# One core of Trainium2, hybrid decoder step: order of the first page and modulation loads

## What is computed

```python
def adaln_modulation(c, w_ada, b_ada):
    m = jnp.einsum('nd,de->ne', jax.nn.silu(c), w_ada) + b_ada
    return jnp.split(m[:, None, :], 6, axis=-1)

# decoder_layer, shortened
shift_m, scale_m, gate_m, shift_f, scale_f, gate_f = adaln_modulation(c, lw['w_ada'], lw['b_ada'])
h = rmsnorm(x, lw['g_norm_mix']) * (1.0 + scale_m) + shift_m
p = jnp.einsum('ntd,de->nte', h, lw['w_in'])
...
# mla_sample: keys of the cached pages and their norms
c_all = jnp.concatenate([pool_c[pages_i].reshape(PAST_LEN, KV_LORA), c_i], axis=0)
k = mla_keys(c_all, kr_all, w_uk, g_qk_k)      # k_nope = c_kv @ w_uk, then RMSNorm per head
...
x = x + gate_m * merged @ w_out
x = x + gate_f * moe_ffn(rmsnorm(x, g_norm_ffn) * (1 + scale_f) + shift_f)   # 64 experts, top 8, and one shared
```

## Time and profile before

| | us |
|---|---|
| median of 3 runs | 1010.48 (1009.39 to 1010.88) |
| the profiled execution | 1010.36 |
| its span in the profile | 1008.6 |
| TensorE busy | 972.6 (96%) |
| VectorE busy | 610.6 (61%) |
| ScalarE busy | 188.0 (19%) |
| DMA, moved | 311.86 MB, mean 309 GB/s |

### The profile page before, as it was taken

How to read it: one execution, slowest core, us unless ns; L and a number is a source line. 1 busy time by engine, 2 the same in 40 slices (tenths; PEclk the granted TensorE clock), 3 DMA queues, 4 the chain that set the end, 5 groups by cost and what they waited for, 6 DMA issues and landing times.

```text
span 1008.6 us, 14072 instructions
## 1 busy us (share of the span) xinstructions
PE 972.6 (96%) x4542; PEld 547.3 (54%) x4542; DVE 610.6 (61%) x1563; ACT 188.0 (19%) x385; POOL 56.6 (6%) x81
## 2 busy tenths in 40 slices
PE   6999999999999999999999999999999999999997
PEld 2487766444447788888744344444444444344443
DVE  3513322468754011123749889889888888888875
ACT  3311231335435100002510010000000000000000
POOL 0100010000000000000210000000000000000000
PEclk9999999999999999999999999999999999999999
DMA  8994469655545483544569999999999999999991
GB/s 314 421 402 186 175 228 322 180 164 169 162 125 235 160 356 132 209 159 176 214 244 415 425 424 424 426 421 419 423 428 422 422 427 420 425 422 421 422 393 61
DMA packets 54921, 311.86 MB, mean 309 GB/s; under 512 B 8922, under 2 KB 28410, under 8 KB 32978
## 3 DMA queue, kind: packets, MB, share of 16 engines
q1 hardware_dynamic: 48546, 297.21, 74.0%
q0 software_dynamic: 6320, 13.93, 3.9%
HBM read 315.80 MB, written 3.95 MB: 317 GB/s over the span
## 4 chain that ended last, share of the span: by engine, by line
PE 73%; DMA 20%; DVE 3%; issue 1%; SPq 1%; ACT 0%; DVEq 0%; PEldq 0%
PE bank L747 48%; DMA ring<-in_w_e_gu 18%; PE pA L747 17%; PE pB L747 4%; PE pC L747 3%; DMA pT<-in_poolT 1%; PE pD L747 1%; PE pA L782 1%; DMA ring<-in_w_br 0%; PE pA L991 0%; SPq L592 0%; DVE xT L2327 0%; PE pC L1000 0%; PE bank L1315 0%; DVE xT L2403 0%
## 5 line engine op out<-in xcount | busy, mean ns | idle before, releaser
L747 PE MATMUL pA<-ring,qT 128*64 128x512 f32 x992 | 226.8, 595 | 11.1 <-DMA ring<-in_w_e_gu 11.0
L2315 DVE STREAM_TRANSPOSE qT<-xs 32x256 f32<-32x256 f32 x480 | 209.2, 436 | 7.7
L747 PE MATMUL bank<-hT,ring 128*128 128x264 f32 (+1 forms) x832 | 189.3, 388 | 0.9 <-PE bank L747 0.9
L747 PEld LDWEIGHTS bank<-hT,ring 128*128 128x128 f32 (+1 forms) x832 | 154.3, 189 | 34.4 <-issue 8.7
L747 PEld LDWEIGHTS pA<-ring,qT 128*64 128x64 f32 x992 | 74.0, 137 | 137.7 <-issue 128.8
L747 PE MATMUL bank<-pT,vtok 128*128 128x264 f32 x512 | 127.9, 393 | 0.3 <-DVE pT L2407 0.3
L747 PEld LDWEIGHTS bank<-pT,vtok 128*128 128x128 f32 x512 | 92.0, 190 | 39.3 <-issue 26.7
L2324 DVE TENSOR_TENSOR pT<-pT,bank 128x264 f32<-128x264 f32 x248 | 99.9, 427 | 8.8 <-PE bank L747 7.3
L747 PE MATMUL bank<-wuk,ring 128*128 128x512 f32 x192 | 86.3, 597 | 0.0
L747 PE MATMUL pB<-ring,oaT 128*64 128x512 f32 x244 | 62.0, 605 | 0.0
L747 PE MATMUL pC<-ring,oaT 128*64 128x512 f32 x244 | 60.3, 592 | 0.0
(11 more groups left out here) (344 smaller groups left out, 795.0 us busy)
## 6 DMA issues: line engine op xcount, KB each, us to landing
ring<-in_w_e_gu SPq DMA_DIRECT2D x62, 2048.0 KB, 18.9
ring<-in_w_e_dn SPq DMA_DIRECT2D x61, 1024.0 KB, 18.6
ring<-in_poolT SPq DMA_DIRECT2D x64, 208.0 KB, 2.7
ring<-in_w_ada SPq DMA_DIRECT2D x12, 1024.0 KB, 9.6
ring<-in_w_bg SPq DMA_DIRECT2D x4, 3072.0 KB, 11.6
ring<-in_w_mix SPq DMA_DIRECT2D x5, 2048.0 KB, 8.7
ring<-in_w_ada SPq DMA_DIRECT2D x4, 2048.0 KB, 12.5
ring<-in_poolR SPq DMA_DIRECT2D x56, 128.0 KB, 2.1
```

What stands on the lines that cost most here:

```text
L747: return nc.tensor.matmul(out, lhsT, rhs, start=start, stop=stop)
L2315: last = V.transpose(xTs[32 * j:32 * j + 32, q % 2, :, 32 * a:32 * a + 32], src[32 * a:32 * a + 32, j])
```

## The change

The first half of modulation chunk 0 (4 of its 8 blocks, 1 MB) is issued ahead of SyncE's wait for the page table and counts on the semaphore of page 0, together with w_uk; the second half goes out after pages 0 to 5, and alone counts on `wgt[0]`. Page groups become {0}, {1}, {2, 3}, {4, 5}, {6, 7}, {8 to 11}, {12 to 15}. Banks follow a table of their own (`EBANK`), as the groups of pages no longer fit the stages. On TensorE, ScalarE and VectorE pages 4 and 5 move ahead of chunk 0 and of the norm's square and tile sums.

```diff
-EGROUP = (0, 1, 4, 6, 8, 10, 12, 16)
+EGROUP = (0, 1, 2, 4, 6, 8, 12, 16)
+EBANK = (0, 4, 6, 8, 10, 12)
...
-STAGES = [("ek0", 1), ("ek1", 3), ("ada0", 1), ("ek4", 2), ("ek6", 2), ("norm1", 1), ("ada1", 1), ("ek8", 2), ("ada2", 1),
+STAGES = [("ek0", 4), ("ek4", 2), ("ada0", 1), ("ek6", 2), ("norm1", 1), ("ada1", 1), ("ek8", 2), ("ada2", 1),
...
 def early_bank(e):
-    g = max(x for x in EGROUP if x <= e)
+    g = max(x for x in EBANK if x <= e)
...
             def ada_item(x):
+                if x == 0:
+                    sp.dma_start(part(0, CT * 512, CT, 512), A["w_ada"][0][:, CT:DT]).then_inc(wgt[0], 16)
+                    return
...
             sp.dma_start(wuk, A["w_uk"]).then_inc(d_early[0], 16)
+            sp.dma_start(part(0, 0, CT, 512), A["w_ada"][0][:, 0:CT]).then_inc(d_early[0], 16)
             sp.wait_ge(d_ptab, 16)
-            early_pages(0)
-            early_pages(1)
+            for g in range(4):
+                early_pages(g)
             ada_item(0)
             sp.dma_start(xT[:], A["xT"]).then_inc(d_in, 16)
             sp.dma_start(vec[:], A["vec"]).then_inc(d_in, 16)
-            early_pages(2)
-            early_pages(3)
+            early_pages(4)
             ada_item(1)
-            early_pages(4)
+            early_pages(5)
             ada_item(2)
-            early_pages(5)
             early_pages(6)
             ada_item(3)
...
                     if e in EGROUP:
                         g = EGROUP.index(e)
-                        pe.wait_ge(d_early[g], 16 * (EGROUP[g + 1] - e + (g == 0)))
+                        pe.wait_ge(d_early[g], 16 * (EGROUP[g + 1] - e + 2 * (g == 0)))
...
-            early_keys(0, 2)
-            early_keys(2, 4)
+            early_keys(0, 6)
             pe.wait_ge(s["csilu"], 1)
             pe.wait_ge(d_late, 16)
             ada_item(0)
-            early_keys(4, 6)
             pe.wait_ge(s["consts"], 6)
             early_keys(6, 8)
...
-            early_squares(0, 4)
+            early_squares(0, 6)
             ada_rows((0,))
             act.wait_ge(d_in, 16 * 2)
             nc.scalar.activation(sq[:], xT[:], ACT.Square).then_inc(s["sq1"], 1)
-            early_squares(4, 8)
+            early_squares(6, 8)
...
-            early_sums(0, 4)
+            early_sums(0, 6)
             dve.wait_ge(s["sq1"], 1)
             tile_sums(rstd[:], sq[:])
-            early_sums(4, 8)
+            early_sums(6, 8)
```

## The result

The changed kernel takes 1014.68 us (median; 1012.66 to 1016.16) against 1010.18 us of the kernel before in the same runs: ratio 1.0042, 95% interval 1.0031 to 1.0054, so it is 4.5 us slower. The forecast was 1014.2 us, 1011.6 to 1017.2. The profiled execution took 1015.02 us, its span is 1013.3 us.

A forecast was written before the change was run, and what follows sets the result against it. Bound: TensorE (73% of the span), its data waits overtaken by the norm's chain at 32.87 us. Chunk 0 at 20.9 + 10.0 + 5.8 = 36.7 at ada_fold(1), +3.8; 1010.36 + 3.8 = 1014.2 us, range 1011.6 to 1017.2.

The forecast's parts named there:

- First page: TensorE's first matmul, behind the half chunk in the queue: 8.5 us instead of 5.74, bounds 7.8 and 9.2.
- The reckoning by bytes: For page 0's landing: 1.18 MB left at 5.00 us, taking 2.9 us at 407 GB/s or 3.9 at 303.
- TensorE until chunk 0: Six pages from the first matmul, 0.4 us for the clock: chunk 0 starts at 20.9 us instead of 15.08.
- gauge: Start of ada_fold(1) on TensorE, 32.87 us before the change: a shift there is a shift of the end.
- Norm chain: Square of xT and tile sums behind chunk 0: new 3.0 us wait before the column sum, scaling at +10.0.
- rival A: TensorE's clock falls in the new 3.0 us wait before the column sum, costing 1.7 us: shift +5.3, 1015.7; chance 0.28.
- the likeliest case: Clock stays at 2.4 GHz through the new wait: ada_fold(1) at 36.7, +3.8 us, 1014.2; chance 0.50.
- Propagation: After ada_fold(1): everything later is released by work behind it, so all is displaced by as much, +3.8 us.
- rival B: Waits for expert weights, 11.0 us in all, shrink by 3.8 us and take up the slip: 1010.4; chance with D 0.14.
- D: Every effect is hidden under the queue of the first 85 us: 1010.5; chance with rival B 0.14.
- Rival C: First page still lands at 5.7 us and the norm isn't last; page 7 ends 2.7 us early: 1007.7; chance 0.04.
- Range: Whole time 1011.6 to 1017.2 us: low end below the forecast's, up to rival A's with the late start.

The follow-up runs named there:

- the repeat: The changed kernel run again with no edit, beside a kernel with filler matmuls in the new wait: 1014.42 us, ratio 1.0045 to the kernel before.
- order alone: The changed kernel with modulation chunk 0 in one piece after pages 0 to 5 again, no half ahead: 1013.33 us against 1010.28, ratio 1.0031.
- the better order: Changed kernel without the half ahead, xT behind page 3 in the queue, norm's square and tile sums ahead of pages 4 and 5: 1008.62 us, ratio 0.9985.
- the last experiment: The better order plus matmuls on constants ahead of page 0, with page 6 also moved ahead of chunk 0 on TensorE and ScalarE: 1010.11 us, ratio 1.0003.

## Why the prediction was right, point by point

- *First page:* 8.5 us forecast, 8.26 measured. That it is the queue, not the semaphore, is shown by the run with the half on a count of its own. The reckoning by bytes held, with one term off: from 3.10 to 5.00 the DMA engines did not move the 308 GB/s of before but 397, as the first of the windows above shows.
- *TensorE until chunk 0:* 20.9 forecast, 20.18 measured; 0.24 of it is the first page, the rest the six pages, which took 11.9 us here and 12.4 in the repeat (12.4 forecast, 0.4 of it for the clock). That the pages' own semaphores bring next to nothing fits the run with them alone, whose times can't tell 0.9 us from nothing and whose gauge did not move forward.
- *Norm chain:* the scaling L1790 was to follow chunk 0 by 10.0 us and did; the wait before the column sum was to be 3.0 us, ended by the tile sums, and was 2.70. The kernel with the norm detached shows that this chain makes most of the loss; the half chunk alone makes 1.56 us.
- *Forecast or rival A:* the price of the likeliest case was +3.8 at `ada_fold(1)`, with the clock held. The chip did what rival A says, in all four traces that have this wait (the change twice, order alone, half on its own count). A's 38.2 us at the gauge stands against 38.45 and 38.01. So I gave the clock's fall too small a chance, 0.28, where it seems to be the rule; the step of the working that failed is the clock held at 2.4 GHz through the new wait, for which one fall at the end of the kernel had been taken for a weak sign. In the sum, the way from L1790 to `ada_fold(1)` was put at 5.8 us and took 8.27 (30.18 to 38.45), while chunk 0 came 0.7 us earlier than forecast. Rival A's price for the fall, 1.7 us, lies between the 1.4 and the 2.7 us of the two traces. That the predicted 1014.2 is near the measured median in spite of this is luck: at the gauge the slip was 5.6 and not 3.8 us, and 1.2 us of it are missing at the end because the kernel before happened to wait that much more in the experts' stage of its trace. The Trainium skill ("TensorE: Matmul & The Clock Gate", HAM oscillation) has the waits between bursts put the array back to the lower clock; these traces agree that a wait can do so, and here 2.70 us were enough, less than the waits of the page's example.
- *Propagation:* 5.4 us at 85 us and 5.6 at 600: nothing takes the slip up (rival B and D), and most of the gain of the better order stays too: 1.26 us at the gauge, 1.0 at 600 us, 1.9 at the end (spans of 1006.7 and 1008.6), where the wait of the kernel before named above is in it. Rival C did not occur: with the half ahead of it, page 0 started TensorE at 8.26 to 8.65 us in six traces.
- *Range:* its upper end of 1017.2 does not follow from the terms. Rival A's +5.3 with the start 0.7 us later gives 1010.36 + 6.0 = 1016.4. The lower end, 1011.6, is likewise a choice: the lowest bound that was worked out, +2.7, gives 1013.1.

## What to carry to other kernels

A wait for data that an engine shows may be slack for another chain: before moving work into it, list what is queued behind the moved work on every engine, and count to the point where the chains meet. Here the tile sums are ready some 8.6 us after the start of chunk 0. In the kernel before, TensorE had chunk 0, four pages and the wait of 1.67 us until the column sum, in all 10.5 us, and so never noticed; the change left it chunk 0 and two pages, 5.9 us. The edit that pays is to start that chain before the reordered work. What is put ahead in a transfer queue delays the small transfers behind it (here 1 MB made a page 2.5 us late), and an order changed on the engines has to be changed on the queue as well.

## What I had not expected of the hardware

- With an idle time of 2.68 to 2.70 us TensorE's clock fell to 1.2 GHz in each of four traces, in two of them within the wait and in two (order alone, half on its own count) some 0.3 us after its end; 1.67 us in the kernel before and 1.77 us in the last experiment left it at 2.4 GHz. The lower clock lasted until 35 us in one trace though TensorE was busy from 28.8, and until 33 in another.
- The same six pages from the first matmul to chunk 0 took 11.9, 12.4, 12.8 and 13.2 us in different executions, by how many of the first matmuls were 0.85 us apart and not 0.43, which I read as the lower clock (the granted clock of the profile reads 1.00 even there); with matmuls on constants ahead they took 11.0.
